# Unit 0 of a two-layer streaming encoder: its stages put in another order on every engine, with other banks and load orders

## What is computed

```python
for layer in range(2):
    h = rms_norm(x, norm_mix)
    p = h @ w_in                       # 1536 attention, 256 state-space, 896 RWKV columns
    y_A = diff_attention(p_A)          # 4 heads, QK-norm, partial rotary, two softmaxes, rms_norm
    y_B = s5_mixer(p_B)                # diagonal complex scan, gelu, sigmoid gate, rms_norm
    y_C = rwkv7_mixer(p_C)             # delta-rule state, token by token, group norm, gate
    x = x + concat(y_A, y_B, y_C) @ w_out
    h = rms_norm(x, norm_ffn)
    q = (h @ w_q)                      # 8 heads x 2 halves x 128
    s = q . sub_keys                   # 128 keys a half; top 16 of each, top 16 of the 256 sums
    x = x + sum_k softmax(best)_k * gelu(u_tab[expert_k] . h) * v_tab[expert_k]
```

## Time and profile before

| | |
|---|---|
| runs, median | 1849.26, 1846.55, 1834.77 us; 1846.55 |
| profiled execution | 1863.27 us; its span (first to last instruction) 1861.2 us |
| PE busy | 1388.1 us, 75% |
| DVE busy | 1410.9 us, 76% |
| POOL busy | 1235.0 us, 66% |
| ACT busy | 379.0 us, 20% |
| DMA | 640.89 MB, 344 GB/s over the span |
| of them the gathers' queue | 538.25 MB, 76.5% of 16 engines' span |

### The profile page before, as it was taken

How to read it: one execution, slowest core, us unless ns; L and a number is a source line. 1 busy time by engine, 2 the same in 40 slices (tenths; PEclk the granted TensorE clock), 3 DMA queues, 4 the chain that set the end, 5 groups by cost and what they waited for, 6 DMA issues and landing times. The chain is left out here.

```text
span 1861.2 us, 17527 instructions
## 1 busy us (share of the span) xinstructions
PE 1388.1 (75%) x5274; PEld 804.2 (43%) x5274; DVE 1410.9 (76%) x3371; ACT 379.0 (20%) x926; POOL 1235.0 (66%) x1090
## 2 busy tenths in 40 slices
PE   6688669877876849868966968966987736655567
PEld 5465645344545535335535553434555312222222
DVE  6763799999666699998768598997766875785553
ACT  2331222223211221312210222321121111100100
POOL 6000585788754576687785667777775777787775
PEclk9777879989988979989888979999998969887879
DMA  7313999999999999999999999999999999999998
GB/s 220 110 59 113 340 382 400 407 377 336 379 398 383 345 325 394 388 353 353 391 393 392 371 353 392 382 349 362 397 391 340 373 357 368 353 339 341 366 378 320
DMA packets 222865, 640.89 MB, mean 344 GB/s; under 512 B 18570, under 2 KB 72692, under 8 KB 222772
## 3 DMA queue, kind: packets, MB, share of 16 engines
q0 software_dynamic: 147920, 538.25, 76.5%
q1 hardware_dynamic: 74604, 101.48, 15.9%
q10 hardware_dynamic: 248, 0.04, 0.0%
HBM read 638.65 MB, written 1.05 MB: 344 GB/s over the span
## 5 line engine op out<-in xcount | busy, mean ns | idle before, releaser
L547 POOL DMA_INDIRECT arena<-in_peer_u_dram,expert x512 | 605.7, 1183 | 355.7 <-DVE expert L1538 156.8
L1571 DVE SCALAR_TENSOR_TENSOR arena<-arena,normed 128x1024 f32<-128x1024 f32 x512 | 615.2, 1225 | 211.0 <-DMA arena<-in_peer_u_dram,expert 204.6
L547 POOL DMA_INDIRECT arena<-in_peer_v_dram,expert x512 | 598.7, 1169 | 244.1 <-issue 142.6
L2029 PE MATMUL bank<-arena,diag 128*128 128x512 f32 x768 | 451.1, 672 | 257.5 <-DMA arena<-in_peer_v_dram,expert 177.2
L2030 PE MATMUL bank<-arena,diag 128*128 128x512 f32 x768 | 426.6, 639 | 0.0
L2029 PEld LDWEIGHTS bank<-arena,diag 128*128 128x128 f32 x768 | 143.7, 209 | 470.5 <-issue 386.5
L1626 PE MATMUL bank<-h_cm,wring 128*128 128x128 f32 x1536 | 214.3, 308 | 69.7 <-DMA wring<-in_peer_w_q_dram 52.9
L2030 PEld LDWEIGHTS bank<-arena,diag 128*128 128x128 f32 x768 | 159.9, 208 | 211.8 <-issue 211.8
L1626 PEld LDWEIGHTS bank<-h_cm,wring 128*128 128x128 f32 x1536 | 210.0, 223 | 83.1 <-DMA wring<-in_peer_w_q_dram 38.2
L1575 DVE SCALAR_TENSOR_TENSOR x<-arena,weight,x 128x1024 f32<-128x1024 f32 x128 | 164.6, 1286 | 40.1 <-DMA arena<-in_peer_v_dram,expert 38.0
L911 ACT ACTIVATE diag<-ident,weight 128x128 f32<-128x128 f32 x384 | 129.7, 391 | 217.7 <-DVE weight L1581 117.7
(11 more groups left out here) (417 smaller groups left out, 1374.2 us busy)
## 6 DMA issues: line engine op xcount, KB each, us to landing
wring<-in_w_in_dram SPq DMA_DIRECT2D x40, 1024.0 KB, 12.6
wring<-in_peer_w_q_dram SPq DMA_DIRECT2D x32, 1024.0 KB, 20.9
wring<-in_w_out_dram SPq DMA_DIRECT2D x16, 1024.0 KB, 9.2
arena<-in_peer_u_dram,expert POOLq DMA_INDIRECT x512, 6.7
arena<-in_peer_v_dram,expert POOLq DMA_INDIRECT x512, 6.6
wring<-in_w_in_dram SPq DMA_DIRECT2D x4, 512.0 KB, 6.8
x<-in_x_dram SPq DMA_DIRECT2D x2, 512.0 KB, 6.9
gain_ffn<-in_norm_ffn_dram SPq DMA_DIRECT2D x2, 512.0 KB, 8.7
```

The source lines that it names most:

```text
L547: nc.gpsimd.indirect_dma_start(out=rows[g % RING], out_offset=None, in_=tables[kind], in_offset=bass.IndirectOffsetOnAxis(ap=expert[:, n % ...
L1571: ins = stt(row, row, 1.0, hb, ALU.mult, ALU.mult, accum_out=dots[:, slot:slot + 1])
L2029: mm(bank[6][:, :], d, row[:, 0:512], start=first, stop=end)
```

## The change

Only the order and the places of work change; what is computed is the same, and every gather and table entry too. For unit 0:

- SP loads its eight vectors ahead of `bc0`; POOL holds the loads of `s_c` back until `h_cm` is written.
- PE does `bc2`, `bc3`, `bc4` ahead of the transposes for the b matrices; the c transposes follow at once. `lora` comes ahead of `da0`; `da4` and `da5` come right behind `da3` and go to bank 3.
- DVE splits `setup_input`: the small factors stay early (`setup_factors`), the part that needs the b matrices comes behind the RWKV inputs. `products` comes ahead of `s5_turn(0)`; both scans come ahead of the masks; `score_max` ahead of level 1; the steps of the attention and the state-space mixer move one or two levels up; `attended` and `s5_skip` go ahead of the last addition.
- ACT loads the tanh table before the data is there, and the Exp table after the square root; `softmax` moves to level 1, `o_squares` and `o_roots` one level up.
- PE does `out0` and `s5_glu` between level 6 and `rhs`, `out1` behind `y`; all four groups of key transposes at once, into four banks.

For all units `lora` multiplies the low-rank inputs first and the squares of k last (one semaphore, `kk_ps`, goes), and the key transposes go to four banks.

```diff
             sp.dma_start(x[:, 0, :], xv[0]).then_inc(s_x[0], 16)
-            load(0, BC_NAMES[0])
             for name, k in VECTORS[0::2]:
                 vector(sp, name, k)
+            load(0, BC_NAMES[0])
...
+            pool.wait_ge(hT_v, 1)
             for i, name in enumerate(("ssm_c_re", "ssm_c_im")):
...
+                if n == 0:
+                    own(A_(small_a[:, 30:31], eps[:, 0:1], ACT.Tanh))
                 act.wait_ge(cc_ok, n + 1)
...
                 if n == 0:
+                    lora()
+                    kk_length()
+                    own(A_(small_a[:, 30:31], eps[:, 0:1], ACT.Exp))
+                    decays()
                     input_map()
-                    lora()
-                    decays()
-                    kk_length()
-                    output_map()
                     squares()
                     qk_lengths()
-                if n:
-                    values()
+                values()
...
                     masks()
-                    setup_input()
+                    setup_factors()
+                    lambda_sums()
...
                 if n:
                     s5_scan(0)
+                else:
+                    setup_input()
                 yield "da4"
...
-                    lambda_sums()
                     decay()
+                    products()
                     dve.wait_ge(st_turns, 1)
                     s5_turn(0)
-                    products()
...
+                if n == 0:
+                    score_max((0, 1))
                 for k in range(1, LEVELS):
...
+                    if n == 0 and k == 6:
+                        attended()
+                        s5_skip()
                     yield f"d{k}"
...
                     if n == 0:
-                        if k == 1:
-                            s5_scan(1)
+                        if k == 2:
+                            s5_back_re()
                         if k == 3:
-                            s5_back_re()
-                        if k == 4:
                             s5_back_im()
                         if k == 5:
-                            s5_skip()
+                            o_scale()
...
                 if n == 0:
                     pe.wait_ge(z_ok, 2)
-                    to_rows(n, "da4", 7)
+                    score_pair(0)
+                    score_pair(1)
...
-                    if n == 0 and k == 2:
-                        to_rows(n, "da5", 7)
...
                     if n == 0:
+                        if k == 3:
+                            attend()
                         if k == 4:
-                            pe.wait_ge(v_ok, 1)
-                            attend()
+                            o_length()
+                            s5_output((0,))
                         if k == 5:
-                            o_length()
-                            s5_output()
+                            s5_output((1,))
+                        if k == 6:
+                            pe.wait_ge(mix_d, 1)
+                            to_model(n, "out0")
+                            s5_glu()
...
                 if t == 0:
-                    turn_keys(0)
-                    turn_keys(1)
+                    for i in range(4):
+                        turn_keys(i)
...
                         if t == 0:
-                            pe.wait_ge(key_ok, 4 * layer + 2)
-                            turn_keys(2)
-                            turn_keys(3)
+                            pe.wait_ge(key_ok, 4 * layer + 4)
```

More of the change, by code:

```diff
@@ L863, in peer @@
                 if t == 0:
[L864 to L867 removed]
+                    for i in range(4):
+                        if i < 3:
+                            act.wait_ge(key_ps, 3 * layer + i + 1)
+                        else:
+                            chunk_used(act, n, "keys")
+                        A_(keys_cm[:, 4 * i:4 * i + 4, :], quad((4, 5, 0, 1)[i]), ACT.Copy).then_inc(key_ok, 1)
+                    act.wait_ge(key_ok, 4 * layer + 4)
                 yield "q0"
@@ L988, in setup_angles, with setup_factors @@
                 dve.wait_ge(st_ang, 1)
-            def setup_input():
+            def setup_factors():
                 dve.wait_ge(st_trig, 1)
-                dve.wait_ge(st_fill, 1)
-                dve.wait_ge(st_b, 1)
-                for ri in range(2):
-                    for q in range(2):
-                        ps_ = slice(64 * q, 64 * q + 64)
-                        own.add(V.tensor_copy(b_raw[ps_, ri], bank[6 + ri][ps_, :].rearrange("p (h a q) -> p a h q", a=16, q=2)[:, :, :, q]))
                 are, aim, den, cr, ci, tmp = (s5p[:, i, :] for i in range(6))
@@ L1014, in setup_input @@
                 own(tt(ci, ci, den, ALU.mult))
-                crb, cib = (a.unsqueeze(2).broadcast_to([P, 16, GCH]) for a in (cr, ci))
+            def setup_input():
+                dve.wait_ge(st_fill, 1)
+                dve.wait_ge(st_b, 1)
+                for ri in range(2):
+                    for q in range(2):
+                        ps_ = slice(64 * q, 64 * q + 64)
+                        own.add(V.tensor_copy(b_raw[ps_, ri], bank[6 + ri][ps_, :].rearrange("p (h a q) -> p a h q", a=16, q=2)[:, :, :, q]))
+                dve.wait_ge(s_dve, own.count)
+                crb, cib = (s5p[:, i, :].unsqueeze(2).broadcast_to([P, 16, GCH]) for i in (3, 4))
                 own.add(tt(b_t[:, 0], crb, b_raw[:, 0], ALU.mult))
@@ L1669, in s5_output @@
                         pe.wait_ge(st_done, 1)
-                    for hf in range(2):
+                    for hf in halves:
                         for b in range(4):
@@ L1787, in mixing @@
                 last.then_inc(chunk_done, 1)
+                if n == 0:
+                    pe.wait_ge(s_b, 16 * B_LOADS)
+                    for ri in range(2):
+                        flat = b_flat[ri][0:32, :].rearrange("p (a h) -> p a h", h=GCH)
+                        for h in range(GCH):
+                            last = tr(bank[6 + ri][:, 32 * h:32 * h + 32], flat[:, :, h], ident[0:32, 0:32])
+                    last.then_inc(st_b, 1)
+                    pe.wait_ge(raw_ok, 3)
+                    pe.wait_ge(s_c, 16 * C_LOADS)
+                    for i in range(4):
+                        for ri in range(2):
+                            last = tr(quad((1, 4)[i // 2])[:, 2 * (i % 2) + ri, :], c_raw[:, ri, i, :], ident[:, :])
+                    last.then_inc(st_cps, 1)
                 yield "da0"
                 pe.wait_ge(raw_ok, 3 * n + 2)
+                if n == 0:
+                    lora()
                 to_rows(n, "da0", 3 if n else 0)
@@ L1796, in mixing @@
                     last.then_inc(st_bps, 1)
-                if n == 0:
-                    lora()
-                    s5_input(0)
                 yield "da1"
                 to_rows(n, "da1", 3 if n else 0)
-                if n == 0:
-                    pe.wait_ge(raw_ok, 3)
-                    pe.wait_ge(s_c, 16 * C_LOADS)
-                    for i in range(4):
-                        for ri in range(2):
-                            last = tr(quad((1, 4)[i // 2])[:, 2 * (i % 2) + ri, :], c_raw[:, ri, i, :], ident[:, :])
-                    last.then_inc(st_cps, 1)
                 yield "da2"
@@ L1821, in mixing @@
                     pe.wait_ge(z_ok, 2 * n + 2)
-                if n:
                     lora()
-                if n:
-                    to_rows(n, "da4", 1)
+                else:
+                    pe.wait_ge(kk_sd, 1)
+                to_rows(n, "da4", 1 if n else 3)
+                if n == 0:
+                    s5_input(1)
                 yield "da5"
-                if n:
-                    to_rows(n, "da5", 1)
+                to_rows(n, "da5", 1 if n else 3)
                 yield "sy"
```

105 lines of the change are left out of this document (44 added, 61 removed).

## The result

Over 22 runs each, the changed kernel took 1836.91 us (median; 1828.19 to 1857.83) and the kernel before 1849.41 us (1830.2 to 1861.44). That is 12.5 us less by the medians and 9.5 us by the averages. The ratio is 0.9947, 95% interval 0.9925 to 0.9969.

The account below looks back on a forecast made before the run. The prediction saw a chain of about 199 us in unit 0, then a DMA-bound stream of 1662 us. Its terms (-10.3 - 2.5 + 4.8 - 1.4 - 2.2 - 1.8 = -13.4) took 1846.55 to 1833 us, range 1829 to 1838.

Parts of the forecast that it names:

- Two things in a row: Whole kernel: a chain of about 199 us in unit 0, then a 1662 us stream; chain savings come off the end.
- Start, -4.1: Kernel start: vectors loaded ahead of `bc0` let PE begin at 9.5 instead of 13.67 us, 4.1 us earlier.
- To the low-rank matmuls: Up to `lora`: b transposes, DVE's wait and table load leave the path (3.7, 4.7, 1.3 us); `lora` starts at 38.3.
- Attention columns, -10.3: Up to the masks: six `da` chunks behind `lora`, both scans ahead of the masks, which begin at 78.6, not 88.9.
- a sign against it: Ahead of the first gather: `da` chunks waiting for weights would show the prediction wrong.
- Level 2, -2.5: Level 2: without `da5` the update begins right behind its product's copy, 2.5 us earlier.
- the clock hurts: Levels 2 and 5 and `out0`: PE at 1.2 GHz loses 9 us, giving 1842 us; chance 0.14.
- Level 6, +4.8: Last product to `rhs`: reciprocal, product into `mixed`, `out0` and gate matmuls now stand between, 4.8 us longer.
- `rhs` to `y`, -1.4: Between `rhs` and `y`: gate matmuls, tanh and squares are done earlier, saving 1.4 us, between 0 and 2.5.
- `var`, -2.2: At `var`: it no longer waits behind an `out` chunk once its input is ready, saving 2.2 us.
- keys, -1.8: Ahead of `q0`: two groups of key transposes move into PE's wait for the norm, saving 1.8 us.
- The sum, -13.4: Whole chain: all terms together bring the first gather to 185.5 us and the time to 1833 us.

Follow-up runs that it names:

- e5_same: The changed kernel run again unaltered, beside the kernel before: 1905.35 us, ratio to before 0.9956.
- e6_delay: The changed kernel with eight extra DVE reciprocals (14.27 us) ahead of the first expert indices: 1917.68 us.
- e10_same: The changed kernel unaltered, a third time: 1839.06 us, ratio to before 0.9946.
- e12_delay3: The changed kernel with 24 extra DVE reciprocals (42.87 us) ahead of the first expert indices: 1876.03 us.
- e7_start: The kernel before with only the start changed (vectors ahead of the first weight block, loads of c later): 1906.73 us, ratio 0.9946.
- e1_pause: The changed kernel with POOL pausing its table doubling until DVE has finished `cc`: 1884.35 us, ratio to before 0.9903.
- e8_best: The changed kernel with POOL's pause, the second scan in level 1 and ACT copying k: 1892.36 us, ratio to before 0.991.
- e3_scan: The changed kernel with the second state-space scan moved from ahead of the masks into level 1: ratio to before 0.9927.
- e9_before: The kernel before, unaltered, profiled once more: profiled execution 1849.27 us, ratio against itself 0.996.
- e2_level6: The changed kernel with the last level's order put back as before: ratio to before 0.9956.
- e4_all: The changed kernel with POOL's pause, the last level as before and the second scan in level 1: 1878.33 us, ratio 0.9887.
- e11_best: The same kernel as e8_best, run for a second interval: 1831.71 us, ratio to before 0.9939.

## Why the prediction was right, and where it wasn't

*Two things in a row.* Right within the spread. The delays of 14.3 and 42.9 us reached the end as 12.3 and 37.0, and the DMA share of the stream stayed as it was: 0.96 in `e5_same` and `e6_delay`, 0.99 and 0.98 in `e10_same` and `e12_delay3`.

*Start, -4.1.* Right: -4.3 in the changed kernel, and -3.4 to -3.9 down the chain in `e7_start`.

*To the low-rank matmuls.* Right in what leaves the path; a term was missed. The sum put `lora_in` at 37.8; it came at 40.6 + 1.1 = 41.7. I had read in the earlier trace rows that DVE's products are slow beside POOL's doubling, and asked whether they would still be slow in their new place. I did not ask what would now stand beside the doubling instead: `cc`, 4.7 us longer, on the path. `e1_pause` shows the cause. The Trainium skill (SBUF — State Buffer, Who interferes with whom) lets a DVE operation with two SBUF inputs and a GpSimd one that reads SBUF exclude each other. The trace agrees: a `cc` operation takes 6.67 / 7 = 0.95 us on average beside POOL operations of 0.7 to 1.3 us, and 1.93 / 7 = 0.28 alone. The rule was in the prediction, applied to the instruction that moved and not to the one that moved into its place.

*Attention columns, -10.3.* Measured -6.1 to -7.4. With the pause the masks stand at 78.24 and 78.04 against 78.6 forecast, so the missing 3 to 4 us are those of `cc`. That this meets the forecast so closely is partly luck, as the timeline of `e1_pause` shows:

```profile
68.45 1.04 PE L1859 MATMUL bank<-ident,work 128*128 128x128 f32 x8
...
71.45 0.69 DVE L1089 TENSOR_TENSOR arena<-arena 128x512 f32<-128x512 f32 x1
72.18 0.69 DVE L1227 COPY kT<-bank 128x512 f32<-128x512 f32 x1
72.90 5.30 DVE L1098 TENSOR_TENSOR_SCAN arena<-mag,arena 128x128 f32<-128x128 f32 x16
```

PE reached the transposes of q and k at 68.45, 2.1 us ahead of the forecast 70.5. But from there the copy of k came 3.7 us later and not 2.0, because `s5_turn(1)` stands ahead of it on DVE, which the sum left out. `e8_best`, with that copy on ACT, has the masks at 74.6. The working also named the scans as last; `e3_scan` shows PE's products as late as they when they run at 1.2 GHz. And in the changed kernel one `da` chunk did wait for its weights, which the forecast had named as a sign against it, but only for 0.6 us.

*Level 2, -2.5.* Mis-sized. The second and the third copy of a product in the changed kernel, and the third of before (the second stands in the earlier trace rows):

```profile
97.69 0.60 ACT L821 ACTIVATE work<-bank 128x512 f32<-128x512 f32 x1 [2.28 <-PE bank L1896]
104.52 0.60 ACT L821 ACTIVATE work<-bank 128x512 f32<-128x512 f32 x1 [6.24 <-PE bank L1896]
```

```profile
112.99 0.60 ACT L817 ACTIVATE work<-bank 128x512 f32<-128x512 f32 x1 [2.50 <-PE bank L1881]
```

From the one to the other it takes 6.83, 6.75 and 7.03 us in the changed kernel's three profiles and 7.97 in both of before: -1.1. The other profiles agree, 6.8 to 7.3 us in all that have the new order and 7.97 in `e7_start`. Without `da5` the update's pairs of passes take 0.63 us, against 0.39 behind it in before (the earlier trace rows has 0.38 at 108.20). So the mechanism of the rival *the clock hurts* is there, at 1.5 us in this level, and not the 9 us that the rival gave it over three places. The Trainium skill (TensorE: Matmul & The Clock Gate, What's actually happening) has the slow clock as the default and activity as what releases it; this level agrees (0.63 us a pair without the large matmul, 0.39 behind it).

*Level 6, +4.8.* Measured +6.4 where `out0` began at 1.2 GHz (5.40 us), and +4.8 in `e10_same`, where it took 3.70: `rhs` at 130.36, 7.44 us behind the product's copy, against 2.69 in before. The term is right at the fast clock.

*`rhs` to `y`, -1.4; `var`, -2.2; keys, -1.8.* Right: -1.9, -2.2, and -1.7 from `var` to `q0` between the first two profiles.

*What was no term.* Between the first two profiles, the levels 3 to 5 took 3.1 us less (18.5 against 21.5, from the third copy of a product to the sixth), the wait from `y`'s copy to `mean` 1.9 less, and `q0` to the gather 2.0 less (16.4 against 18.4). `e9_before` has 19.0 for the levels, 3.4 for the wait, where the first profile of before had 5.3 and the changed kernel 3.3, and 17.2 for the last; `e5_same` has 17.5, 4.2 and 18.1. So most of it is the clock of one execution, not the change. They nearly hid what was mis-sized, and the gather at 184.20 looked like the forecast 185.5: that was luck.

*The sum, -13.4.* With the averages of the three profiles of the changed kernel and the two of before, the terms come to -6.6 (masks) - 1.1 + 5.5 - 1.7 - 2.2 - 2.1 = -8.2 us. The averages of many runs give -9.5, -8.4 and -10.7 in three groups, the medians -12.5, -7.7 and -7.2. So the mechanism of the forecast holds, and its size, 13.4, was some 3 to 5 us too large: about 4 for `cc`, 1.4 in level 2 and 0.7 in level 6, against 0.6 that `rhs` to `y` and the keys gave beyond their terms. By the medians of 22 runs alone the gain was 12.5 against 13.4 forecast, which looks better than it was; of the 3.9 us between the time and the forecast, 2.9 are the median of before, which rose from 1846.55 to 1849.41 with more runs.

What stays open: how the clock shifts the average of the chain behind the masks. Three chains of before and five of the changed kernel can't tell a mean from luck there. Nor was the move of `da5` undone alone, since its output bank is taken by the scores in the new order.

## What to carry to other kernels

When slow instructions are moved away from the engine that slows them, look at what comes to stand beside that engine, and price it as slow: contention stays where its cause is. In this kernel a chain ahead of a saturated stream passed its microseconds on nearly one for one, but its length has to be read from several executions, as one profile of this kernel was 10 us longer than another behind the same point. A load that is moved into a wait pays only as far as the later waits couldn't have held it, and it is worth looking up which engine is second when the first is relieved.

## What the runs showed of the hardware

Beside GpSimd's doubling even a DVE `tensor_scalar` with one 64x128 input took 1.12 us instead of 0.22, in the three of the changed kernel's chains in which it began before POOL's last operation was through (changed, `e2_level6`, `e10_same`); it ended within 0.1 us of that operation. It is not so each time: with the pause (`e1_pause`, `e4_all`, `e8_best`, `e11_best`) it began 0.14 to 0.15 us before the end of a POOL operation and took 0.22 or 0.23, while the two `tensor_scalar` behind it, again beside POOL, took 0.97 together instead of 0.48. I had expected only operations with two inputs to suffer. The Trainium skill (SBUF — State Buffer, Who interferes with whom) says that a `tensor_scalar` can take a mode with two ports and then contends as well; the slow cases agree, though no run here shows in which mode it was.

TensorE's two rates came at different places in executions of the same kernel: the 20 pairs of passes of `y` took 4.8 us once and 8.4 another time, the 32 of `q0` 3.8 or up to 5.8. With the same instructions in the same order, the chain behind the masks differed by 10.4 us in the kernel before and by 4.9 in the changed one.
